# Reordered first loads, shared input scaling, regrouped gate activations and alternating row halves in a streamed two-block model

## What is computed

```python
def reference(x, ..., mem_2, w_in_2, ...):
    x = first_block(x, norm_w, w_in, ...)      # x + sigmoid(ga) * (mlstm @ w_out) + sigmoid(gb) * (deltanet @ w_out)
    return second_block(x, mem_2, w_in_2, ...)

# first block, the parts the change touches
h = rmsnorm(x) * norm_w
i_pre = softcap(ml_i + ml_i_bias)
logf = log_sigmoid(softcap(ml_f + ml_f_bias))            # softcap(t) = 15 tanh(t / 15)
beta = sigmoid(dn_b)
g = -exp(dn_a_log) * softplus(dn_a + dn_dt_bias)

# second block, GLA of one chunk: decays between rows i and j
decay = exp(-abs(b[:, None] - b[None, :]))               # b = cumsum(log gates)
attn = einsum('bihd,bjhd,bijhd->bhij', q, k, decay)
```

## Time and profile before

| | |
|---|---|
| median of 3 runs | 2302.64 us (2302.16 to 2303.63) |
| profiled execution | 2303.89 us |
| its span, first to last instruction | 2302.2 us |
| mean granted TensorE clock | 0.990 |
| TensorE busy | 2235.0 us, 97% |
| VectorE busy | 1275.7 us, 55% |
| ScalarE busy | 1119.2 us, 49% |
| GpSimd busy | 124.8 us, 5% |
| DMA | 399 MB, mean 173 GB/s |

### The profile page before, as it was taken

How to read it: one execution, slowest core, us unless ns; L and a number is a source line. 1 busy time by engine, 2 the same in 40 slices (tenths; PEclk the granted TensorE clock), 3 DMA queues, 4 the chain that set the end, 5 groups by cost and what they waited for, 6 DMA issues and landing times.

```text
span 2302.2 us, 32811 instructions
## 1 busy us (share of the span) xinstructions
PE 2235.0 (97%) x12407; PEld 1848.3 (80%) x12407; DVE 1275.7 (55%) x1457; ACT 1119.2 (49%) x1505; POOL 124.8 (5%) x172
## 2 busy tenths in 40 slices
PE   7999999999999999999999999999999999999995
PEld 6788888888888778878888878887887788778884
DVE  4445456464545647484755554466545845556455
ACT  6445445454445647383745454444443544444433
POOL 5000000000000101001010000000000200000002
PEclk9999999999999999999999999999999999999998
DMA  6765655656566545353545755645557466445552
GB/s 218 223 214 169 194 175 164 205 182 202 192 183 183 147 125 151 104 173 111 164 129 179 246 172 176 197 133 152 158 184 265 134 226 189 133 145 164 184 192 101
DMA packets 213991, 399.22 MB, mean 173 GB/s; under 512 B 21048, under 2 KB 37555, under 8 KB 212960
## 3 DMA queue, kind: packets, MB, share of 16 engines
q1 hardware_dynamic: 205664, 365.61, 51.7%
q0 software_dynamic: 5616, 21.23, 2.8%
q10 hardware_dynamic: 2576, 10.49, 1.3%
HBM read 388.82 MB, written 8.45 MB: 173 GB/s over the span
## 4 chain that ended last, share of the span: by engine, by line
PE 87%; ACT 4%; issue 3%; DVE 3%; DMA 2%; POOL 1%; DVEq 0%; SPq 0%; ACTq 0%; POOLq 0%
PE stream_psum L548 25%; PE stream_psum L550 25%; PE stream_psum L549 25%; PE heads_psum L714 3%; PE heads_psum L526 3%; ACT w_high L967 1%; PE heads_psum L891 1%; ACT work L967 1%; DMA w_raw<-in_w_mem_kv 1%; DMA w_raw<-in_w_in 1%; PE heads_psum L854 1%; PE heads_psum L833 1%; ACT L967 1%; DVE work L1549 1%; PE heads_psum L722 1%
## 5 line engine op out<-in xcount | busy, mean ns | idle before, releaser
L1383 DVE TENSOR_TENSOR w_low<-w_raw,w_high 128x1024 fp32r<-128x1024 f32 (+1 forms) x700 | 836.2, 1211 | 756.4 <-ACT w_high L967 754.8
L967 ACT ACTIVATE w_high<-w_raw 128x1024 fp32r<-128x1024 f32 (+1 forms) x700 | 715.4, 1047 | 479.9 <-PE stream_psum L550 395.0
L548 PE MATMUL stream_psum<-w_high,x_high 128*128 128x512 f32 x1856 | 744.8, 401 | 6.7 <-ACT proj L967 3.0
L550 PE MATMUL stream_psum<-w_high,x_low 128*128 128x512 f32 x1856 | 725.4, 391 | 0.0
L549 PE MATMUL stream_psum<-w_low,x_high 128*128 128x512 f32 x1856 | 725.0, 391 | 0.0
L548 PEld LDWEIGHTS stream_psum<-w_high,x_high 128*128 128x128 f32 x1856 | 349.9, 189 | 82.6 <-issue 6.3
L550 PEld LDWEIGHTS stream_psum<-w_high,x_low 128*128 128x128 f32 x1856 | 349.5, 188 | 74.6
L549 PEld LDWEIGHTS stream_psum<-w_low,x_high 128*128 128x128 f32 x1856 | 350.1, 189 | 69.4 <-issue 1.9
L548 PE MATMUL stream_psum<-w_high,y_high 128*128 128x512 f32 x896 | 355.6, 397 | 10.0 <-DVE w_low L1383 7.9
L550 PE MATMUL stream_psum<-w_high,y_low 128*128 128x512 f32 x896 | 350.1, 391 | 0.0
L549 PE MATMUL stream_psum<-w_low,y_high 128*128 128x512 f32 x896 | 349.9, 391 | 0.0
(11 more groups left out here) (276 smaller groups left out, 1290.1 us busy)
## 6 DMA issues: line engine op xcount, KB each, us to landing
w_raw<-in_w_in SPq DMA_DIRECT2D x528, 512.0 KB, 4.5
w_raw<-in_w_out SPq DMA_DIRECT2D x128, 512.0 KB, 4.8
w_raw<-in_w_mem_kv SPq DMA_DIRECT2D x32, 512.0 KB, 5.0
work<-rows_scratch POOLq DMA_DIRECT2D x8, 512.0 KB, 6.2
proj<-in_mem SPq DMA_DIRECT2D x2, 1024.0 KB, 7.9
residual<-in_x ACTq DMA_DIRECT2D x1, 2048.0 KB, 12.7
mkv_scratch<-proj POOLq DMA_DIRECT2D x4, 512.0 KB, 4.5
mem_high_scratch<-y_high POOLq DMA_DIRECT2D x4, 512.0 KB, 4.0
```

Source lines behind the costliest of these rows:

```text
L548: pe.matmul(acc, hi[:, k, sl(m)], w, start=first, stop=False)
L550: last = pe.matmul(acc, lo[:, k, sl(m)], w, start=False, stop=final)
L967: return act.activation(dst, src, func, **kw)
L1383: tt(WL[:, c % RING, 0:width], RAW[:, c % RING, 0:width], WH[:, c % RING, 0:width].bitcast(F32), ALU.subtract).then_inc(lo_done, 1)
```

## The change

- The memory is loaded in four quarters of its columns, each waited for by itself. x is loaded by the SyncE queue in two halves of its rows, behind weight chunks 1 and 2, in the place of one load from ScalarE's queue.
- Before its first feature ScalarE runs a one-column copy. The high halves of chunks 0 and 1 come before memory features 4 and 6, the low halves after low features 3 and 5. In the first block of the stream TensorE waits with each chunk for the features of that chunk only.
- In `x_prep` the squares, the roots and the scaling are spread over more chunks; ScalarE scales the first row of x in two pieces and VectorE the second. The transposes of x come two half chunks later.
- In `gates` the three exponentials run before the two logarithms, and TensorE's cumulative sums come four half chunks later, the steps of the other engines to match.
- In `pairs` the innermost loop goes over the two halves of the partitions.

The diff without the lines that only renumber a semaphore:

```diff
--- before.py
+++ after.py
@@ -152,8 +152,9 @@
-        consts, small_in, x_in = sem("consts"), sem("small_in"), sem("x_in")
-        mem_in = [sem(f"mem_half{i}_in") for i in range(2)]
+        consts, small_in, x_scaled = sem("consts"), sem("small_in"), sem("x_rows_scaled")
+        mem_in = [sem(f"mem_quarter{i}_in") for i in range(4)]
+        x_in = [sem(f"x_rows{m}_in") for m in range(M)]
         cols_pe, cols_v = sem("cols_transposed"), sem("cols_copied")
@@ -170,7 +171,7 @@
         W_GATE = 4 * 48
-        G_ACT = steps_of(sem("gates_act"), ["mini", "tanh", "expf", "lnf", "expab", "lnab", "alog", "eg", "eb",
+        G_ACT = steps_of(sem("gates_act"), ["mini", "tanh", "expf", "expab", "alog", "lnf", "lnab", "eg", "eb",
                                          "hb", "kd", "emt"])
@@ -331,11 +332,13 @@
-            for i in range(2):
-                sp.dma_start(PR[:, :, sl(i, D // 2)], mem2[:, :, sl(i, D // 2)]).then_inc(mem_in[i], 16)
+            for i in range(4):
+                sp.dma_start(PR[:, :, sl(i, D // 4)], mem2[:, :, sl(i, D // 4)]).then_inc(mem_in[i], 16)
             for half in range(2):
...
                     put(N_MEM, half * NCH + c, rows_in_chunk(w_mkv, half * NBLK, 1024, c, [[1, NBLK]]))
+                    if half == 0 and c in (1, 2):
+                        sp.dma_start(RES[:, c - 1, :], x2[:, c - 1, :]).then_inc(x_in[c - 1], 16)
             narrow(N_GATE, w_in, 0, IN1, [(C_IF, 16), (C_BA, 32)])
@@ -525,7 +528,7 @@
-            def stream(n, blocks_before, nblk, hi, lo, side, first_need=None, tiles=tuple(range(0, KT, CH)), small=None):
+            def stream(n, blocks_before, nblk, hi, lo, side, first_need=None, tiles=tuple(range(0, KT, CH)), small=None, features=None):
@@ -538,6 +541,8 @@
                         i = b * per + c
+                        if features and b == 0:
+                            pe.wait_ge(features, c + 1)
                         pe.wait_ge(lo_done, n + (i + 1))
@@ -567,13 +572,13 @@
-            def feature_tiles(src, count, through, before, ready=None, second=None):
+            def feature_tiles(src, count, through, before, ready=None, parts=None):
...
                         pe.wait_ge(count[0], count[1] * (c - 3) + before)
-                    if second and c == NCH // 2:
-                        pe.wait_ge(*second)
+                    if parts and c % 2 == 0:
+                        pe.wait_ge(parts[c // 2], 16)
                     if ready:
@@ -595,9 +600,9 @@
                 tr(H[:, 0, 226:228], wk(8.75, P)[0:2, :], 2).then_inc(cols_pe, 1)
-                yield from gap(9)
+                yield from gap(11)
                 pe.wait_ge(cols_v, 5)
-                pe.wait_ge(norm_s, 5)
+                pe.wait_ge(x_scaled, M)
                 yield from feature_tiles(wk(0, 4 * U).rearrange("p (m d) -> p m d", m=M), (x_lo, 2), x_pe, 0)
@@ -605,7 +610,7 @@
                 last.then_inc(*signal(G_PE, "gt"))
-                yield from gap(5)
+                yield from gap(9)
                 pe.wait_ge(*done(G_V, "g"))
@@ -884,9 +889,9 @@
-                    for par in range(2):
-                        for hh in range(2):
-                            for i, (ms, mt) in enumerate(tiles):
+                    for hh in range(2):
+                        for i, (ms, mt) in enumerate(tiles):
+                            for par in range(2):
                                 r = slice(64 * par, 64 * par + 64)
@@ -918,11 +923,9 @@
-            pe.wait_ge(mem_in[0], 16)
             pe.wait_ge(consts, 2)
-            finish(feature_tiles(PR, (m_lo, 1), m_pe, 0, second=(mem_in[1], 16)))
-            pe.wait_ge(m_lo, NCH)
-            stream(N_MEM, E_MEM, 2, YH, YL, x_prep())
+            finish(feature_tiles(PR, (m_lo, 1), m_pe, 0, parts=mem_in))
+            stream(N_MEM, E_MEM, 2, YH, YL, x_prep(), features=m_lo)
             pe.wait_ge(evac, 2 * E_ML)
@@ -1003,24 +1006,24 @@
             def x_prep():
-                yield from gap(3)
                 act.wait_ge(m_lo, NCH)
-                act.wait_ge(x_in, 16)
                 for m in range(M):
+                    yield from gap(2)
+                    act.wait_ge(x_in[m], 16)
                     f(wk(4, D), RES[:, m, :], ACT.Square, accum_out=ST[:, m:m + 1]).then_inc(norm_s, 1)
                     act.wait_ge(norm_s, m + 1)
-                yield
+                yield from gap(2)
                 f(ST[:, 2:4], ST[:, 0:2], ACT.Ln, scale=1.0 / D, bias=eps_c).then_inc(norm_s, 1)
...
                 f(ST[:, 4:6], ST[:, 2:4], ACT.Exp, scale=-0.5).then_inc(norm_s, 1)
+                yield from gap(2)
                 act.wait_ge(norm_s, 4)
-                yield from gap(2)
-
                 act.wait_ge(cols_v, 5)
-                for m in range(M):
-                    last = f(wk(2 * m, D), RES[:, m, :], ACT.Copy, scale=ST[:, 4 + m:5 + m])
-                last.then_inc(norm_s, 1)
-                yield from gap(5)
+                for h in range(2):
+                    last = f(wk(h, U), RES[:, 0, sl(h, U)], ACT.Copy, scale=ST[:, 4:5])
+                    yield
+                last.then_inc(x_scaled, 1)
+                yield from gap(4)
                 for c in range(NCH):
@@ -1033,14 +1036,13 @@
                 f(LG[:, :, 0:8], TI[:, :, 8:16], ACT.Exp, scale=-15.0).then_inc(*signal(G_ACT, "expf"))
-                act.wait_ge(*done(G_ACT, "expf"))
-                f(LG[:, :, 0:8], LG[:, :, 0:8], ACT.Ln, bias=1.0).then_inc(*signal(G_ACT, "lnf"))
                 act.wait_ge(*done(G_V, "negabs"))
                 f(NA[:], NA[:], ACT.Exp).then_inc(*signal(G_ACT, "expab"))
+                f(EA[:], BIA[:, 32:48], ACT.Exp).then_inc(*signal(G_ACT, "alog"))
                 act.wait_ge(*done(G_ACT, "expab"))
+                f(LG[:, :, 0:8], LG[:, :, 0:8], ACT.Ln, bias=1.0).then_inc(*signal(G_ACT, "lnf"))
                 f(NA[:], NA[:], ACT.Ln, bias=1.0).then_inc(*signal(G_ACT, "lnab"))
-                f(EA[:], BIA[:, 32:48], ACT.Exp).then_inc(*signal(G_ACT, "alog"))
-                yield from gap(6)
+                yield from gap(10)
                 act.wait_ge(*done(G_V, "kd"))
@@ -1264,14 +1266,12 @@
             act.wait_ge(eps_ready, 1)
+            f(ST[:, 46:47], eps_c, ACT.Copy)
             for c in range(NCH):
-                if c == NCH // 2:
-                    act.wait_ge(mem_in[1], 16)
-                    act.dma_start(RES[:], x2).then_inc(x_in, 16)
+                if c in (4, 6):
+                    high(N_MEM, c // 2 - 2, 0)
                 act.wait_ge(m_pe, c + 1)
                 f(YH[:, 2 * c:2 * c + 2, :], H[:, c % 4:c % 4 + 1, :].rearrange("p b (j t) -> p (b j) t", j=2), ACT.Copy).then_inc(m_hi, 1)
-            for c in range(AHEAD):
-                high(N_MEM, c, 0)
             stream(N_MEM, 2, 0, x_prep(), ahead=(W_GATE, EX_GATE))
@@ -1413,7 +1413,13 @@
                 dve.tensor_copy(NC_[:, 33:35], H[:, 0, 226:228]).then_inc(cols_v, 1)
-                yield from gap(8)
+                yield from gap(4)
+                dve.wait_ge(norm_s, 4)
+                for h in range(2):
+                    yield
+                    last = ts(wk(2 + h, U), RES[:, 1, sl(h, U)], ST[:, 5:6], None, ALU.mult)
+                last.then_inc(x_scaled, 1)
+                yield from gap(4)
                 for c in range(NCH):
@@ -1430,13 +1436,14 @@
                 stt(NA[:], GT[:, :, 16:48], -1.0, GT[:, :, 16:48], ALU.mult, ALU.min).then_inc(*signal(G_V, "negabs"))
-                dve.wait_ge(*done(G_ACT, "alog"))
+                yield from gap(5)
+                dve.wait_ge(*done(G_ACT, "lnab"))
...
                 stt(LG[:, :, 8:24], GT[:, :, 32:48], -1.0, b3(EA[:]), ALU.mult, ALU.mult).then_inc(*signal(G_V, "g"))
-                yield from gap(3)
+                yield from gap(2)
                 dve.wait_ge(*done(G_PE, "cumsum"))
@@ -1771,8 +1778,8 @@
                 tt(v(YL), H[:, c % 4:c % 4 + 1, :].rearrange("p b (j t) -> p (b j) t", j=2), v(YH).bitcast(F32), ALU.subtract).then_inc(m_lo, 1)
-            for c in range(AHEAD):
-                low(N_MEM, c)
+                if c in (3, 5):
+                    low(N_MEM, (c - 3) // 2)
             stream(N_MEM, 2, x_prep(), ahead=W_GATE)
```

More of the change, by code:

```diff
@@ L1302, in square_block @@
                     f(wk(4, NBLK), RES[:, m, sl(b, NBLK)], ACT.Square, accum_out=ST[:, 56 + 4 * m + b:57 + 4 * m + b]).then_inc(norm_s, 1)
-                    act.wait_ge(norm_s, 6 + 2 * b + m)
+                    act.wait_ge(norm_s, 5 + 2 * b + m)
             def squares():
@@ L1317, in rms_features @@
                 yield from gap(2)
+                act.wait_ge(norm_s, 13)
+                f(ST[:, 2:4], ST[:, 0:2], ACT.Ln, scale=1.0 / D, bias=eps_c).then_inc(norm_s, 1)
                 act.wait_ge(norm_s, 14)
-                f(ST[:, 2:4], ST[:, 0:2], ACT.Ln, scale=1.0 / D, bias=eps_c).then_inc(norm_s, 1)
-                act.wait_ge(norm_s, 15)
                 f(ST[:, 4:6], ST[:, 2:4], ACT.Exp, scale=-0.5).then_inc(norm_s, 1)
```

(5 more changed lines are left out.)

3 lines of the change are left out of this document (1 added, 2 removed).

## The result

| | before | changed |
|---|---|---|
| median, side by side (4 runs each) | 2303.14 us | 2284.77 us (2283.72 to 2285.96) |
| profiled execution / its span | 2303.89 / 2302.2 us | 2285.96 / 2284.3 us |

The changed kernel takes 0.9919 of the time before (95% interval 0.9905 to 0.9933). The forecast was 2281.4, or 0.9908; the time is 3.4 us above it, inside the range. The profiled executions differ by 17.9 us where the sum said 21.2.

The account below looks back on a forecast made before the run. TensorE, busy 97% of the span, was taken to bound the kernel. The terms -2.9 + 0.8 - 5.4 - 13.7 = -21.2 us took the profiled 2303.9 to 2282.7, set against the median 2281.4; range 2276 to 2290.

Parts of the forecast that it names:

- slide of the gate loads: The narrow gate loads on SyncE's queue slide 0.8 us against TensorE because x's transposes start later: +0.8 us.
- Part 4: GLA pairs at L891: alternating row halves lets products overlap at the delta net's ratio, -13.7 us over two layers.
- at that ratio a group takes 0.82: GLA pairs: sixteen records fall from 1.64 to 0.82 us, as the delta net's go from 67 to 34 ns each.
- Rival (b): GLA pairs overlap only partly, 75 ns a record, gaining 7.3 us: 2287.8 us; chance 0.10.
- (a): GLA pairs don't overlap because 128-column weight loads take turns; only the start is left: 2295.1 us; chance 0.10.
- (d): GLA pairs get slower, each switch of row halves draining the array, 0.25 us each: 2320 us; chance 0.04.
- Part 3: Gates: regrouped table loads and later cumulative sums shrink the 4.0 us stall to about 2 at full clock: -5.4 us.
- the row transposes at about 94.5: Marker behind the gates: the row transposes, at 101.99 us before, would come 7.5 us earlier.
- Part 2: Memory stream: TensorE's stalls before 36.52 and 41.26 us both go, -2.9 us; later gate loads cost +0.8.
- Part 1: First loads: TensorE's stream start stays at 18.6 us; priced at 0, with bounds of -1.6 and +1 us.
- (c): Start: chunk 0 lands by 14.5 us with the clock still up, -1.6 and up to -2.4 more: 2277.4; chance 0.06.
- (e): Start fails: the stall before chunk 3 drops the clock, x lands late, +2.5 and +1.5: 2285.4 us; chance 0.10.

Follow-up runs that it names:

- e4_gates: The kernel before with only the new order of the gates, TensorE's and VectorE's gaps included: 2296.83 us, ratio 0.9977.
- e11_after_again: The changed kernel run once more, unchanged, in a later session: 2282.1 us, ratio 0.9911 to the kernel before.
- e2_rest: The changed kernel with the old loop order of the pairs: 2293.05 us, ratio 0.9961 to the kernel before.
- e3_runs2: The changed kernel with runs of two products (four records) per row half in the pairs instead of one: 2286.57 us.
- e8_xlast: e7_split with the second row of x loaded behind chunk 3 instead of chunk 2: 2280.42 us, ratio 0.9904; run again 2280.98, ratio 0.9908.
- e7_split: The changed kernel with one high half put between the exponentials and the logarithms of the gates: 2284.52 us, ratio 0.9916.
- e1_pairs: The kernel before with the new loop order in the pairs as the only edit: 2293.49 us, ratio 0.9961.

## Why the prediction came out as it did

| term | forecast | measured |
|---|---|---|
| start | 0 | -1.9 (0.85 sooner, clock up sooner) |
| stalls before 36 and 41 us | -2.9 | -1.6 |
| slide of the gate loads | +0.8 | 0.0 |
| gates | -5.4 | -5.5 |
| GLA pairs | -13.7 | -8.8 |
| sum | -21.2 | -17.8 |

**Part 4, the pairs: the right mechanism, 4.9 us too much.** The step that failed is "at that ratio a group takes 0.82". Its sixteen records took 1.09. The ratio from the delta net halves everything; here two things don't halve. The old group already overlapped three records, so it was 1.64 and not 1.98, and each half's first step of about 213 ns is paid once in either order. With those the sum is 213 + 6 x 112 = 885 ns to the last pair, 7 more to its second record, and 0.2 us to its end: 1.09. The records of one half stay 112 ns apart. Rival (b), partial overlap at 75 ns a record, had the size (2287.8, group 1.2) but not the cause; rivals (a) and (d) fell, with no trace of a drain in a change of halves at 7 ns. The group of half size, priced at 0.3 us, kept its time. From group to group it is 8.12 us, not 7.9. Chain of waits, changed kernel:

```profile
1562.51 0.65 PE heads_psum L896 x8
```

For rival (a) the prediction took the figure of the Trainium skill (TensorE: Matmul & The Clock Gate, LDWEIGHTS), 107 ns for 128 columns. The trace has 112 ns between records of one row half, close to it; what rival (a) got wrong is that loads of different row halves take turns.

**Part 3, the gates: right.** -5.4 forecast, -5.5 by starts, 5.6 by the median of `e4_gates`. One stall of "about 2 us before chunk 3" was 1.62, with the clock at 1.00, and the two table loads went. The marker was set wrongly, though: "the row transposes at about 94.5" compares unlike places, for in the new order they come two chunks later in TensorE's work, 5.5 us. The place that stood at 101.99 is now 92.99, 9.0 earlier where 7.5 was forecast.

**Part 2, the stalls: half right.** "So both stalls go" failed. ScalarE's chain was even faster than foreseen (chunk 6 at 35.06, not 36.7) and so were VectorE's pieces of x:

```profile
36.21 1.37 DVE L1383 TENSOR_TENSOR w_low<-w_raw,w_high 128x1024 fp32r<-128x1024 f32 x1 [2.92 <-ACT w_high L970]
37.51 1.47 DVE L1420 TENSOR_SCALAR work<-residual,stats 128x1024 f32<-128x1024 f32 x2
```

0.73 us each, not 1.0. But TensorE's need came 1.7 us before the 38.3 of the prediction, for it had started sooner and its clock had come back sooner. What was won at the start was waited away before chunk 6, 1.15 us. The margin of 0.4 us that the prediction called thin held only while the start stayed put; I had priced start and stalls as if they did not hang together. Start and stalls together are -3.5 where -2.9 was forecast; that the sum came out near is the coupling, not the parts. `e11_after_again`, the same kernel, shows it from the other side: its clock was low until 23 us, there was no wait before chunk 6, and the row transposes came at 98.53 again. "No wait of TensorE for a low half between 24 and 60 us" was wrong.

**Part 1, the start.** 17.73, inside "between 17 and 19.6", chunk 3's landing at 24.99 inside "23 to 25.5". The slide of +0.8 cost nothing. SyncE's queue in the changed kernel:

```profile
56.75 10.65 SPq L330 DMA_DIRECT2D w_raw<-in_w_in  x16
```

It begins 2.84 sooner than in the earlier trace rows, where TensorE is 3.5 ahead, so there is a slide of 0.6. But the loads take 10.65 instead of 11.88 and end 4.1 sooner, and TensorE keeps its 3.5 through this stage. That the loads would be shorter was not foreseen.

**The other rivals.** (c) came half true in other executions: chunk 0's high half starts at 13.19 in `e2_rest` and 13.15 in `e3_runs2`, but the clock fell at 16.3 in both, and at the row transposes 0.2 and 0.6 us of it were left. (e) fell with the clock at 1.00 over the stall before chunk 3.

The sum of starts between the gates and the end holds, besides the pairs, the drops of the clock near 850 (a loss) and 1745 (a loss in before that the changed kernel was spared). In this pair of executions they cancel: +1.9 from the gates to the first GLA, -1.75 between the two, -0.1 behind them, and the two GLA stages by themselves show as -8.9.

## What to carry to other kernels

- Price an interleaving from the starts of single records in the order that is there, not from a ratio of two other groups: look for overlap that the old order already has, and for what is paid once a group.
- When several stalls lie in a row on one stream, an earlier start moves every later need forward. Recompute the next deadline with the new start before calling a stall gone; here the repair was one load moved behind the weight chunk on which the chain hangs (`e8_xlast`; 1.1 to 4.3 us with the repair of the gates, by session).
- Between exponentials and logarithms, group by table first and then put the waiting engine's next weight chunk between the groups (1.6 us by starts in `e7_split`; its median does not show it).

## What the runs showed of the hardware

- A float32 product of 64 rows by 128 columns starts a record every 112 ns within one half of the rows. One of the other half starts 4 to 13 ns behind it; the gain over no overlap at all is 1.98 / 1.09 = 1.8. The Trainium skill (TensorEngine Tiling (Array Packing), Theoretical Speedup) gives up to 2 for this.
- A half's second record starts about 213 ns after its first instead of 112.
- The clock stood at 1.00 over stalls of 1.62 and 1.41 us. In the changed kernel it was at 0.50 from 14 us on; there TensorE had paused 1.98 us in the transposes (up to 12.69) and worked 1.2 between that and the wait for the stream. In `e11_after_again`, without the pause, it fell in the microsecond from 16 (the first line below) and was still low in that from 21, and the stalls behind took up the difference. Near 1745 us it dropped behind waits of 2.4 us (before), of 2.8 (`e7_split`) and of 2.3 (`e1_pairs`), and not behind one of 2.2 (changed), 2.5 (`e11_after_again`) or 2.7 (`e3_runs2`).
- With the same code of the start, ScalarE's first high half began between 13.15 and 15.27 us. A start can't be judged from one execution; a place behind its last stall can.

```profile
16.00:17.00 1.00, 0.00 (x0) 0.00 (x0) 1.00 (x1) 1.00 (x3) 0.96 (x1) 0.78 1.04 418
...
21.00:22.00 1.00, 1.00 (x4) 0.81 (x3) 0.95 (x1) 0.02 (x1) 0.87 (x3) 0.50 1.05 393
```
